# Two transformer blocks on one core: the second block's token mixer spread between the tiles of its projections

## What is computed

```python
px = hx @ w_in[l]                    # 1696 columns: f, cb, cc, cx, q, kv, kr
kn, kr, v = mla_kv(px[..., OFF_KV:], kv_norm[l], w_ukv[l], cos, sin)
qn, qr = mla_q(px[..., OFF_Q:OFF_KV], q_norm[l], w_uq[l], cos, sin)
att = attend_blocked(qn, qr, keys of x and context, values of both)
f  = fft2(px[..., :256]).real        # over tokens and features
cv = cb * conv(cc * cx, conv_w)      # three taps
xs = xs + gate * (concat([f, cv, att]) @ w_out[l])
```

## Time and profile before

| | us |
|---|---|
| median of three runs (2720.78 to 2724.14) | 2722.24 |
| the profiled execution | 2721.82 |
| its span | 2720.0 |
| PE busy | 2507.4 (92%) |
| DVE busy | 1846.3 (68%) |
| ACT busy | 1099.7 (40%) |
| mean granted clock of TensorE | 0.963 |

### The profile page before, as it was taken

One profiled execution on the slowest core, in us unless ns is written; L12 is line 12 of the kernel. 1 busy time (PEld: TensorE's weight loads), 2 busy tenths in 40 slices (PEclk: granted clock), 3 DMA queues, 4 the chain that ended last, 5 costly groups with the idle time before them and its releaser, 6 DMA issues.

```text
span 2720.0 us, 37566 instructions
## 1 busy us (share of the span) xinstructions
PE 2507.4 (92%) x15010; PEld 2147.0 (79%) x15010; DVE 1846.3 (68%) x3136; ACT 1099.7 (40%) x1695; POOL 53.3 (2%) x56
## 2 busy tenths in 40 slices
PE   5889999866899799999987899999999999978998
PEld 4849999754799778888875588888888888866997
DVE  2647999644566667787945677676876666866666
ACT  4475447722454532222514452222442222544543
POOL 1010000021000000000000000000000000000000
PEclk8999999988999899999998999999999999988999
DMA  7877996522466546655322036555445554422663
GB/s 260 244 227 202 282 279 181 155 93 78 129 183 186 148 124 171 176 164 166 101 51 72 8 98 166 155 163 157 138 133 157 140 151 124 120 76 60 182 185 109
DMA packets 632563, 407.59 MB, mean 150 GB/s; under 512 B 27751, under 2 KB 588614, under 8 KB 631366
## 3 DMA queue, kind: packets, MB, share of 16 engines
q1 hardware_dynamic: 631712, 404.94, 51.8%
q10 hardware_dynamic: 678, 0.25, 0.0%
HBM read 404.09 MB, written 1.05 MB: 149 GB/s over the span
## 4 chain that ended last, share of the span: by engine, by line
PE 83%; DVE 8%; ACT 4%; DMA 2%; issue 1%; SPq 1%; ACTq 0%; POOL 0%; DVEq 0%; POOLq 0%
PE ps L1562 71%; PE ps L1584 2%; PE ps L1599 1%; PE ps L569 1%; PE ps L833 1%; DMA raw<-in_attn_w_in 1%; PE ps L1336 1%; DVE w_lo L1900 1%; PE ps L843 1%; PE ps L1311 1%; DVE p L1405 1%; DVE stat L1395 1%; DVE tmp L2100 0%; PE ps L1323 0%; DVE ada_acc L1917 0%
## 5 line engine op out<-in xcount | busy, mean ns | idle before, releaser
L1742 ACT CAST w_hi<-raw 128x1024 fp32r<-128x1024 f32 (+3 forms) x557 | 554.7, 997 | 1210.4 <-PE ps L1562 1174.0
L1562 PE MATMUL ps<-h_hi,w_hi 128*128 128x258 f32 (+2 forms) x2952 | 969.4, 328 | 27.2 <-DVE h_lo L2109 13.7
L1562 PE MATMUL ps<-h_lo,w_hi 128*128 128x258 f32 (+2 forms) x2952 | 964.5, 327 | 0.0
L1562 PE MATMUL ps<-h_hi,w_lo 128*128 128x258 f32 (+2 forms) x2952 | 963.6, 326 | 0.0
L1900 DVE TENSOR_TENSOR w_lo<-raw,w_hi 128x1024 fp32r<-128x1024 f32 (+3 forms) x557 | 644.9, 1158 | 256.9 <-ACT w_hi L1742 253.9
L1562 PEld LDWEIGHTS ps<-h_hi,w_hi 128*128 128x128 f32 x2952 | 561.3, 190 | 82.5 <-issue 26.5
L1562 PEld LDWEIGHTS ps<-h_lo,w_hi 128*128 128x128 f32 x2952 | 560.8, 190 | 46.7
L1562 PEld LDWEIGHTS ps<-h_hi,w_lo 128*128 128x128 f32 x2952 | 561.2, 190 | 45.4
L1562 PE MATMUL ps<-a_hi,w_hi 128*128 128x256 f32 (+1 forms) x1056 | 354.6, 336 | 0.5 <-DVE a_lo L1955 0.5
L1562 PE MATMUL ps<-a_lo,w_hi 128*128 128x256 f32 (+1 forms) x1056 | 353.2, 334 | 0.0
L1562 PE MATMUL ps<-a_hi,w_lo 128*128 128x256 f32 (+1 forms) x1056 | 353.2, 334 | 0.0
(11 more groups left out here) (350 smaller groups left out, 2249.0 us busy)
## 6 DMA issues: line engine op xcount, KB each, us to landing
raw<-in_ffn_w_in SPq DMA_DIRECT2D x264, 512.0 KB, 4.6
ada_raw<-in_w_mod SPq DMA_DIRECT2D x120, 512.0 KB, 3.9
raw<-in_ffn_w_out SPq DMA_DIRECT2D x96, 512.0 KB, 5.0
ada_raw<-in_ada_w SPq DMA_DIRECT2D x40, 512.0 KB, 5.4
wide_rows<-in_ada_w SPq DMA_DIRECT2D x40, 512.0 KB, 5.0
raw<-in_ffn_w_out SPq DMA_DIRECT2D x48, 384.0 KB, 3.6
raw<-in_gdn_w_in SPq DMA_DIRECT2D x33, 512.0 KB, 4.1
raw<-in_w_in SPq DMA_DIRECT2D x26, 512.0 KB, 3.9
```

Source lines behind the costliest of these rows:

```text
L1562: last = mm(ps[0:m, slot, 0:n], w[:, slot, k * P:k * P + m], v[:, s0 + k, c0:c0 + n], start=(k == 0 and w is w_hi and v is hi), stop=(k == ...
L1742: nc.scalar.copy(w_hi[:, slot, 0:n], raw[:, slot, 0:n]).then_inc(s_hi, 1)
```

## The change

A table `MIXER_STEPS` gives, for each layer, the order of the 14 blocks of the projection (latents first) and after which tile each step of the mixer is done. The engines do these steps inside the loop over the tiles. The convolution's last product and half of the Fourier products over tokens stay behind the last tile. The three wide tiles of layer 1 move from places 11 to 13 to places 7 to 9. The squares move from DVE to ACT. In layer 1 the roots of q and of kv are taken separately (after tiles 5 and 10), in layer 0 together. A query's rotation goes two tiles behind its query tile, the transposes of a head's values two tiles behind its key and value tile, DVE's and ACT's shares one tile later. The last two transposes stay in `mla`. The first four `w_hi` and three `w_lo` of the output weight move from the `key_value` stage into units 2 to 5 of `mla`. `fm` holds four pairs and no longer two.

```diff
+MIXER_STEPS = (
+    dict(order=(8, 9, 10, 11, 12, 13, 0, 1, 4, 6, 2, 5, 7, 3), kv=3, kr=5, f=6, q_sums=6, kv_sums=6, q_rstd=7, kv_rstd=7,
+         features=(7, 8, 9, 10), turn=8, rope=9, parts={8: (0, 2), 9: (2, 4), 10: (4, 6), 11: (6, 8), 12: (8, 10)}),
+    dict(order=(8, 9, 10, 0, 1, 4, 6, 11, 12, 13, 2, 5, 7, 3), kv=7, kr=9, f=3, q_sums=5, kv_sums=10, q_rstd=6, kv_rstd=11,
+         features=(6, 7), turn=10, rope=11, parts={8: (0, 2), 9: (2, 3), 12: (3, 5), 13: (5, 7)}),
+)
...
+        order = MIXER_STEPS[layer]["order"]
+        parts = ((0, 7, T), (7, 10, 2 * T), (10, 14, T)) if layer else ((0, 14, 2 * T),)
         st += [("norm", "both", ("mla", layer), 2 * T),
-               Linear("mixer_in", ("w_in_2", layer), KD, 11, own, loads=loads[:11], first=0, early="h"),
-               Linear("mixer_in", ("w_in_2", layer), KD, 3, 2 * T, loads=loads[11:], first=11),
+               *(Linear("mixer_in", ("w_in_2", layer), KD, b - a, n, loads=[loads[i] for i in order[a:b]], first=a, early=None if a else "h")
+                 for a, b, n in parts),
...
+        def mixer_step_tensor(pe, lin, t):
             mm = nc.tensor.matmul
+            layer = lin.weight[1]
+            at_, n_s, g0 = MIXER_STEPS[layer], 2 - layer, lin.g0 - lin.more["first"]
+            if t == at_["q_sums"]:
+                pe.wait_ge(event("latents_added"), 3 * layer + 2)
+                mm(ps[:, 7, 0:n_s * T], ones, ssq[:, 0:n_s * T], start=True, stop=True).then_inc(event("latent_sums"), 1)
+            if t == at_["kv_sums"]:
+                pe.wait_ge(event("latents_added"), 3 * layer + 3)
+                mm(ps[:, 6, :], ones, rstd[:], start=True, stop=True).then_inc(event("latent_sums"), 1)
+            if t in at_["features"]:
+                i = at_["features"].index(t)
                 f, c = i % 2, i // 2
+                pe.wait_ge(s_evac, g0 + at_["f"] + f + 1)
                 if i >= 2:
+                    pe.wait_ge(event("fourier_copied"), 4 * layer + i - 1)
                 u = proj2[:, f, c * T:(c + 1) * T]
+                for k in range(NT):
+                    last = mm(ps[:, 4 + f, k * T:(k + 1) * T], u[:, k * P:(k + 1) * P], const("dft_d"), start=True, stop=True)
                 last.then_inc(event("fourier_features"), 1)
+            if t == at_["turn"]:
+                pe.wait_ge(s_evac, g0 + at_["kr"] + 1)
+                pe.wait_ge(event("latent_rstd"), 2 * layer + 1)
+                mm(ps[:, 7, 0:T], const("swap2"), proj2[:, 13, 0:T], start=True, stop=True).then_inc(event("k_rotated"), 1)
+            if t == 12:
+                for i in range(n_s):
+                    fourier_tokens(pe, layer, i)
+            if t == 13:
+                pe.wait_ge(event("latent_rstd"), 2 * layer + 2)
+                pe.wait_ge(event("k_roped"), layer + 1)
+                for i in range(n_s, 2 * n_s):
+                    fourier_tokens(pe, layer, i)
+
...
+        def mixer_step_scalar(act, lin, t):
+            layer = lin.weight[1]
+            at_, n_s, g0 = MIXER_STEPS[layer], 2 - layer, lin.g0 - lin.more["first"]
+            if t in latent_squares(layer):
+                e = latent_squares(layer).index(t)
+                n = n_s * T if e < 3 else 2 * T
+                act.wait_ge(s_evac, g0 + t + 1)
+                if e >= 2:
+                    act.wait_ge(event("latents_added"), 3 * layer + (2 if e == 4 else 1))
+                nc.scalar.activation(sq[:, e % 2, 0:n], proj2[:, at_["order"][t], 0:n], ACT.Square).then_inc(event("latents_squared"), 1)
+            sums = [("q_rstd", n_s * T, 384, ssq, 7, 1), ("kv_rstd", 2 * T, 256, rstd, 6, 2)]
+            sums = [s[1:] for s in sums if at_[s[0]] == t]
+            for n, width, r, bank, count in sums:
+                act.wait_ge(event("latent_sums"), 2 * layer + count)
+                last = nc.scalar.activation(r[:, 0:n], ps[:, bank, 0:n], ACT.Ln, scale=1.0 / width, bias=const("eps"))
+            if sums:
+                link(act, last, "act")
+            for n, width, r, bank, count in sums:
+                nc.scalar.activation(r[:, 0:n], r[:, 0:n], ACT.Exp, scale=-0.5).then_inc(event("latent_rstd"), 1)
+            if t - 1 in at_["features"]:
+                i = at_["features"].index(t - 1)
+                act.wait_ge(event("fourier_features"), 4 * layer + i + 1)
+                nc.scalar.copy(fm[:, i], ps[:, 4 + i % 2, :].rearrange("p (t n) -> p t n", t=NT)).then_inc(event("fourier_copied"), 1)
+            for k in range(*at_["parts"].get(t, (0, 0))):
+                _, dst, c = latent_parts(n_s)[k]
+                n = 10 * layer + k
+                act.wait_ge(event("latent_scaled"), n + 1)
+                nc.scalar.copy(lat_hi[:, dst, cols(c)], tmp[:, n % 4]).then_inc(event("latent_hi"), 1)
...
+            conv_gated(layer, 1)
+            for k in range(*MIXER_STEPS[layer]["parts"].get(13, (0, 0))):
+                latent_lo(dve, layer, k)
+            dve.wait_ge(event("conv_mixed"), 2 * layer + 2)
+
+            def conv_lo(f):
+                dve.wait_ge(event("conv_hi"), 2 * layer + f + 1)
+                return V.tensor_tensor(lo[:, 2 + f, 0:n_s * T], cv[:, f, 0:n_s * T], hi[:, 2 + f, 0:n_s * T].bitcast(F32), ALU.subtract)
+
+            conv_lo(0)
             for i in range(2 * n_s):
...
+        def mixer_step_vector(dve, lin, t):
+            V = nc.vector
+            layer = lin.weight[1]
+            at_, n_s, g0 = MIXER_STEPS[layer], 2 - layer, lin.g0 - lin.more["first"]
+            n = n_s * T
+            if t == 2:
+                dve.wait_ge(event("latents_squared"), 5 * layer + 2)
+                V.tensor_tensor(ssq[:, 0:n], sq[:, 0, 0:n], sq[:, 1, 0:n], ALU.add).then_inc(event("latents_added"), 1)
+            if t == 3:
+                dve.wait_ge(event("latents_squared"), 5 * layer + 3)
+                dve.wait_ge(event("latents_added"), 3 * layer + 1)
+                V.tensor_tensor(ssq[:, 0:n], ssq[:, 0:n], sq[:, 0, 0:n], ALU.add).then_inc(event("latents_added"), 1)
+            if t == at_["kv"] + 2:
+                dve.wait_ge(event("latents_squared"), 5 * layer + 5)
+                V.tensor_tensor(rstd[:], sq[:, 0, :], sq[:, 1, :], ALU.add).then_inc(event("latents_added"), 1)
+            for k in range(*at_["parts"].get(t - 1, (0, 0))):
+                latent_lo(dve, layer, k)
+            for k in range(*at_["parts"].get(t, (0, 0))):
+                latent_scaled(dve, layer, k)
+            if t == at_["rope"]:
+                dve.wait_ge(event("k_rotated"), layer + 1)
+                link(dve, V.tensor_tensor(tmp2[:], ps[:, 7, 0:T], const("sin2"), ALU.mult), "dve")
+                link(dve, V.tensor_tensor(proj2[:, 13, 0:T], proj2[:, 13, 0:T], const("cos2"), ALU.mult), "dve")
+                V.tensor_tensor(proj2[:, 13, 0:T], proj2[:, 13, 0:T], tmp2[:], ALU.add).then_inc(event("k_roped"), 1)
+            if t == 10:
+                dve.wait_ge(s_evac, g0 + t)
+                convolved_rows(dve, layer, 0)
+            if t == 11:
+                dve.wait_ge(s_evac, g0 + t)
+                conv_gated(layer, 0)
+            if t == 13:
+                dve.wait_ge(s_evac, g0 + t)
+                convolved_rows(dve, layer, 1)
...
+        def rotate_query(pe, lin, h):
+
+            L = lin.weight[1]
+            pe.wait_ge(s_evac, lin.g0 + h + 1)
+            if h >= 2:
+                pe.wait_ge(event("q_roped"), 8 * L + h - 1)
+            nc.tensor.matmul(ps[:, 6 + h % 2, 0:T], const("swap2")[0:MLA_QK], qh[0:MLA_QK, h, 0:T], start=True, stop=True).then_inc(event("q_rotated"), 1)
+
...
+        def turn_values(pe, lin, h):
+
+            L = lin.weight[1]
+            pe.wait_ge(s_evac, lin.g0 + h + 1)
+            if h >= 2:
+                pe.wait_ge(event("v_tok2_written"), 8 * L + h - 1)
+            for t in range(4):
+                last = nc.tensor.transpose(ps[:, 4 + h % 2, t * P:(t + 1) * P], kv[:, h, t * P:(t + 1) * P], ident)
+            last.then_inc(event("v2_turned"), 1)
...
+        def values_taken(act, L, h):
+
+            act.wait_ge(event("v2_turned"), 8 * L + h + 1)
+            v = ps[:, 4 + h % 2, :].rearrange("p (t n) -> p t n", t=4)[:, :, DH:P]
+            nc.scalar.copy(v_tok2[:, :, h * DH:(h + 1) * DH], v).then_inc(event("v_tok2_written"), 1)
+            nc.scalar.copy(kv[DH:MLA_QK, h, :], proj2[DH:MLA_QK, 13, :]).then_inc(event("keys_whole"), 1)
...
+        def query_roped(dve, L, h):
+
+            V = nc.vector
+            r = slice(DH, MLA_QK)
+            q = qh[r, h, 0:T]
+            dve.wait_ge(event("q_rotated"), 8 * L + h + 1)
+            V.tensor_tensor(rot2[r, h % 2], ps[r, 6 + h % 2, 0:T], const("sin2")[r], ALU.mult)
+            link(dve, V.tensor_tensor(q, q, const("cos2")[r], ALU.mult), "dve")
+            V.tensor_tensor(q, q, rot2[r, h % 2], ALU.add).then_inc(event("q_roped"), 1)
...
+            kv_lin = stages[stages.index(st) - 1]
+            pe.wait_ge(event("q_roped"), 8 * L + 8)
+            turn_values(pe, kv_lin, 6)
```

(37 more changed lines are left out.)

222 lines of the change are left out of this document (64 added, 158 removed).

## The result

The changed kernel took 2682.35 us (median of 4 runs, 2678.16 to 2683.1), the kernel before 2723.19 us beside it: a ratio of 0.985, 95% interval 0.983 to 0.987. Forecast were 2679 us, range 2666 to 2691. The profiled execution of the changed kernel has a span of 2681.3 us against 2720.0, so 38.7 us are to be found, where the sum of the forecast had 43.4. The medians differ by 40.8 us, since the profiled execution was the slowest of the four.

A forecast was written before the change was run, and what follows sets the result against it. PE, with 83% of the chain of waits, was taken as the bound, improvable only where idle or at half clock. Terms 20.6 + 14.5 + 1.5 + 0 + 12.8 + 2.9 - 6.6 - 2.3 = 43.4 us gave about 2679 us, range 2666 to 2691.

The forecast's parts named there:

- Layer 0, mixer: Layer 0, projection to first query product: first query product at 1422.5 instead of 1443.10, a gain of 20.6 us.
- Layer 0, queries, keys, values: Layer 0, first query product to scores: rotations and transposes between tiles, 0.6 us left behind them; gain 14.5 us.
- Layer 1, projection and mixer: Layer 1 up to the first query product: wide tiles stall 8.6 us, then half clock; gain 0 us.
- Layer 1, queries to scores: Layer 1, query tiles to first scores: DVE becomes the bound, scores at 2433.2 instead of 2446.04; gain 12.8 us.
- The splits: Attention of both layers: three `w_lo` on DVE delay units by 3.3 us a layer, -6.6 us in all.
- Switching: PE changing between kinds of product: 0.08 us lost at each of about 28 places, -2.3 us.
- (a): Whole kernel: the time comes out as summed, 2671 to 2687 us; chance 0.70.
- (b): Layer 1's wide tiles do not stall, as the norm's last blocks come before PE: 2668 us; chance 0.10.
- (c): Both layers: each rotation or transpose waits about 0.5 us for DVE or ACT, +14, 2693 us; chance 0.12.
- (d): ACT's two table loads cost more than their own time, ACT emptying first: 2.6 us, 2682 us; chance 0.03.
- (e): Layer 0: the mixer's last DVE steps still hold the first query, 20.6 us not won, 2700 us; chance 0.02.
- (f): Queries, keys and values of both layers: clock stays at 0.50, costing 59 us, 2738 us; chance 0.03.

The follow-up runs named there:

- e5: Changed kernel with query rotations and value transposes back in a row behind the last key and value tile, as before the change: 2690.5 us, ratio 0.989.
- e8: e5 plus the old coarse wait: first scores wait for value and key row copies of all eight heads. 2698.44 us, ratio 0.991.
- e6: Changed kernel with the eight copies of layer 1's query tiles out of PSUM on ACT instead of DVE: 2678.09 us, ratio 0.984.
- e9: e4 and e6 together, output weight's first splits back between key and value tiles, value copies ahead, no PE wait for latents' root: 2663.58 us, ratio 0.978.
- e4: Changed kernel with layer 1's three 512-wide projection tiles two places later (9 to 11), query root one step later: 2675.61 us, ratio 0.983.
- e2: Changed kernel with layer 1's root of the query latents on ACT one step later, behind the norm's last two roundings: 2682.3 us, ratio 0.985.

## Why the prediction was right, and where it was not

**Layer 0, mixer.** Right, 20.75 against 20.6. The step that carried it was that PE's own 12.5 us at full clock are all that is left between the old end of the projection and the first query product.

**Layer 0, queries, keys, values.** Right in size, 14.36 against 14.5, and right as arithmetic: 33.51 us from the first to the last product stood against 33.9, at a clock of 1.00, without an idle. Of these 14.4 us, e5 and e8 show that at most 7.9 need the rotations and transposes between the tiles. Up to the first probabilities the rest is 7.5 us: 3.9 for the finer waits, and 3.6 for the full clock and the splits that left the key tiles. The prediction put all of it down to the interleaving. Pricing e5 by that term (as measured, 14.4) was what made its expectation fail. A sum against the old gap tells what the change brings, and not which part of it.

**Layer 1, projection and mixer.** Right: 0.35 us lost against 0, an idle of 8.39 against 8.6, a clock of 0.50 behind it. The trace agrees with the table loads as the earlier trace rows had them, 1.28 us and the activation right behind, without a drain on top.

**Layer 1, queries to scores.** This is the term that failed: 12.8 forecast, 7.77 measured, and 5.0 us of it were never there. Two steps of it were wrong. "DVE leaves the mixer 1.2 us after PE": its last mixer step ends 3.5 us after (2379.76, against PE's first query product at 2376.22). The convolution's gate, the last latents' lower parts and the four lower parts of the mixer's output all stand on DVE behind the last tile. In layer 0 I had counted this tail as "some 5 us" and hid it in the ring of tiles, but here there is nothing to hide it, since DVE sets the pace. The second step is what follows DVE's part. PE is tied to DVE only up to the rotation of the last head, at 2394.88, one key tile in. Then come the transposes of six heads at PE's own 1.82 us and the last of them, 11.95 us. I had let DVE's three key iterations run on and put only two key tiles behind them. Of the forecast's 25.6 us (2407.6 to 2433.2) that leaves 9.3 from the same point on, 2.7 too few. The measured path is 3.5 for the tail, 3.0 for three iterations without rotation and the next split, 12.1 to the end of the sixth rotation, 0.1, and 11.95, together 30.6. That DVE becomes the bound, and at 2.15 us a tile, was right, and e6 shows it. The prediction named idle times of PE at a rotation as a sign of being wrong, and here they are. It should have asked for them in layer 1, since PE must wait somewhere once DVE sets the pace.

**The splits.** Right as to mechanism, and in size as far as the clock lets one see, 3.74 and 3.54 against 3.3 a layer. In the changed kernel's attention a pair of units with two splits takes 10.14 us (1473.84 to 1483.98) where it took 8.05 (1507.23 to 1515.28), which is 1.05 a split. At a clock of 1.00 in all, layer 0's attention is 56.20 us in e5, 55.84 in e8 and 53.13 in e9, which is 2.7 to 3.1 for three splits, so some of the 3.74 is clock. In layer 1 the same code gave 3.5 to 5.5 us over the kernel before in six profiles. The move also brought something: PE's extra 2.0 and 1.6 us of wait behind the last key tile are gone. The forecast had them among the 18.5 us behind the tiles and did not name them as the splits'. What it left out is that the splits had a cheap place: in e9, ACT's value copies ahead of them, they cost 0.9 and 0.6 us between the tiles.

**Switching.** Wrong, but small: -2.3 was booked for 28 places. A query tile with its rotation takes 2.53 us in layer 0 and one of each by itself 2.10 and 0.43. A key tile with its transposes takes 1.82, and 1.37 and 0.45 apart. Nothing is lost between them, and layer 0's projection, with mixer products at seven places, came out 0.15 us better than the sum without switching. This error stood against the one in layer 1. That was luck: the median is 3.3 us off the forecast time, and without the booked switching it would have been 5.6. By the stretches of the two profiles the sum is 4.7 off.

**Rivals.** (a) came out as summed. (b) is excluded, since the wide tiles did stall, and e4 shows what they would have been without it. (c) has no row for it in layer 0, where no rotation or transpose waits. In layer 1 the waits of 0.41 to 0.87 us at the rotations are there, but e6 shows them to be DVE's fill and not round trips. (d) is excluded: the activation starts 1.29 us after the load does (2335.47 and 2336.76), which is the load alone. (e) and (f) are excluded by the earlier trace rows against the timeline above and by the clock of 1.00 in both layers' queries.

## What to carry to other kernels

Interleave a small step of one engine with a big one of another only after adding up each engine's whole iteration, with the tail that it still owes from the stage before. Where the sum passes the pace of the bounding engine, move one of its copies to the engine with room, as e6 did. Waits for all heads at a seam are worth replacing by a wait for each head even where nothing is interleaved: here that was 4 us a seam, a part of it through the clock. When a chore is put off to unburden one stage, ask what bounds the stage that it goes to; the order within the old stage (copies that others wait for first, splits last) was most of what it needed.

## What the runs showed of the hardware

- The granted clock in code that no kernel here touches differs from one execution to the next: 0.97 and 0.81 in the same 20 us early in the program, and 5.85 or 7.36 us for the same two tiles in layer 1's projection, at 1.00 or 0.77. Arrivals at one point differed by up to 9 us over ten profiles. For effects below 5 us, the stretch in the trace was a better measure than the total, as long as the clock of the stretch stands beside it: unchanged attention code took 55.8 to 58.4 us.
- After an idle of 4.97 us (e2) the next 2.1 us show a clock of 0.50, and so did the 4.57 us behind an idle of 8.39 us. Behind an idle of 2.19 us (e8, with transposes and short waits before it) the next 5.1 us show 0.50 as well. Where PE did not stall (e4) the wide tiles ran at 1.00.
- PE changes between products of different kinds and shapes without a measurable loss. From the first to the last product of layer 0's queries, keys and values e8 takes 27.75 us and the changed kernel 33.51. The 5.76 between are its eight rotations of 0.43 and five transposes of 0.45 (5.7).
- A table load of ACT takes 1.28 us, and the activation behind it starts within 0.02 us of its end (2335.47, 2336.76).
